# Squares at a layer's end: six of eight blocks added on GpSimd, three tiles summed on TensorE

## The reference

```
def rmsnorm(x, g):
    y = x * rsqrt(mean(x * x, axis=-1) + EPS)
    return y * g

def trunk_layer(x, mod, l, P, ctx):
    h = rmsnorm(x, norm1_g) * (1 + sc1) + sh1
    x = x + g1 * mixer_block(h)
    h = rmsnorm(x, norm2_g) * (1 + sc2) + sh2
    return x + g2 * expert_choice_ffn(h)      # 16 experts, each picks its tokens

y = rmsnorm(x, final_g)                        # after the second layer
```

## Time and profile before

| | us |
|---|---|
| median of 3 runs | 2075.14 (2074.89 to 2081.32) |
| profiled execution | 2075.57 |
| its span (first to last instruction) | 2073.7 |
| TensorE busy | 1896.8 (91%) |
| VectorE, ScalarE, GpSimd busy | 676.0, 378.5, 37.9 |
| end of the first layer: first scatter at 1037.70, q projection starts at | 1051.85 |
| end of the second layer: first scatter at 2054.23, span ends at | 2073.7 |

### The profile page before, as it was taken

How to read it: one execution, slowest core, us unless ns; L and a number is a source line. 1 busy time by engine, 2 the same in 40 slices (tenths; PEclk the granted TensorE clock), 3 DMA queues, 4 the chain that set the end, 5 groups by cost and what they waited for, 6 DMA issues and landing times. The chain is left out here.

```text
span 2073.7 us, 21734 instructions
## 1 busy us (share of the span) xinstructions
PE 1896.8 (91%) x8224; PEld 978.7 (47%) x8224; DVE 676.0 (33%) x1739; ACT 378.5 (18%) x891; POOL 37.9 (2%) x68
## 2 busy tenths in 40 slices
PE   6999989999989899989899999899998998989896
PEld 2445546555544434343354555554655344343432
DVE  1223425544242323231123233353533322232312
ACT  2022312222111110111121223112321011110101
POOL 0000000000000000000000000000000000000000
PEclk9999999999999999999999999999998999999999
DMA  9422341312889999999954214315146899999995
GB/s 362 172 103 102 123 154 61 145 63 102 365 346 428 427 428 427 428 427 428 392 193 163 81 62 147 130 61 188 41 183 263 349 427 427 428 427 428 428 427 216
DMA packets 81655, 547.05 MB, mean 264 GB/s; under 512 B 6992, under 2 KB 10064, under 8 KB 50704
## 3 DMA queue, kind: packets, MB, share of 16 engines
q1 hardware_dynamic: 79104, 536.76, 63.6%
q0 software_dynamic: 2016, 8.06, 1.0%
q10 hardware_dynamic: 432, 0.84, 0.1%
HBM read 541.97 MB, written 3.67 MB: 263 GB/s over the span
## 5 line engine op out<-in xcount | busy, mean ns | idle before, releaser
L865 PE MATMUL bank_D<-HM,ring 128*128 128x384 f32 x1600 | 545.8, 497 | 16.6 <-DMA ring<-w_mgate 4.9
L865 PEld LDWEIGHTS bank_D<-HM,ring 128*128 128x128 f32 x1600 | 302.5, 193 | 235.4 <-issue 38.0
L1310 PE MATMUL bank_D<-ring,HM 128*64 128x512 f32 x912 | 204.8, 596 | 9.8 <-ACT HM L1638 6.6
L871 PE MATMUL bank_D<-ring,HM 128*128 128x512 f32 x384 | 170.1, 597 | 0.0
L1310 PEld LDWEIGHTS bank_D<-ring,HM 128*64 128x64 f32 x912 | 76.0, 138 | 127.7 <-issue 115.6
L1031 PE MATMUL bank_D<-arena_c,ring 128*128 128x384 f32 x384 | 127.3, 488 | 5.0 <-issue 3.1
L871 PEld LDWEIGHTS bank_D<-ring,HM 128*128 128x128 f32 x384 | 71.3, 190 | 86.0 <-issue 84.7
L2226 DVE TENSOR_TENSOR EB<-EB,bank_D 128x512 f32<-128x512 f32 x32 | 22.0, 688 | 267.5 <-ACT EB L1650 267.5
L1334 PE MATMUL bank_Y<-ring,EB 128*64 128x512 f32 x448 | 104.1, 610 | 5.5 <-issue 5.5
L1310 PE MATMUL bank_D<-arena_a,HM 128*64 128x512 f32 x448 | 101.2, 593 | 6.7 <-ACT HM L1638 4.2
L2238 DVE COPY arena_b<-bank_Y 32x512 f32<-32x512 f32 x64 | 44.1, 689 | 176.6 <-PE bank_Y L1334 176.1
(11 more groups left out here) (287 smaller groups left out, 1830.3 us busy)
## 6 DMA issues: line engine op xcount, KB each, us to landing
ring<-ex_w_gate SPq DMA_DIRECT2D x31, 2048.0 KB, 23.2
ring<-ex_w_down SPq DMA_DIRECT2D x28, 2048.0 KB, 19.3
ring<-ex_w_up SPq DMA_DIRECT2D x26, 2048.0 KB, 20.9
ring<-ada_w SPq DMA_DIRECT2D x23, 2048.0 KB, 8.5
ring<-w_in SPq DMA_DIRECT2D x16, 2048.0 KB, 12.7
arena_a<-ex_w_up SPq DMA_DIRECT2D x16, 2048.0 KB, 18.7
arena_a<-ex_w_down SPq DMA_DIRECT2D x15, 2048.0 KB, 23.0
ring<-w_mgate SPq DMA_DIRECT2D x12, 2048.0 KB, 8.1
```

The source lines that it names most:

```text
L865: last = mm(u.t[:, 0:N], w[:, kt, c * P:(c + 1) * P], src[:, kt, :], start=kt == 0, stop=kt == KT - 1)
L871: last = mm(u.t[:, :], HT[:, kt, tile(t)], w[:, kt, 0:CH], start=kt == 0, stop=kt == KT - 1)
L1310: last = mm(u.t[64 * c:64 * c + 64, :], XE[:, h * 4 + k, j, :], w[:, k, c * 512:(c + 1) * 512], start=h == 0 and k == 0, stop=h == 1 and k ...
```

## The change

For the layer's last group the sum steps no longer stand between the scatters: all eight scatters come first, then three sum steps. A new function of GpSimd, add_squares, waits for the second square and adds blocks 0 and 1 into SQ_SUM, then adds blocks 2, 3, 4 and 5 into it, each when its square is done, with a drain between; the last add raises the semaphore pooled. TensorE's first sum step waits for pooled and multiplies SQ_SUM by the ones; the second and third take the blocks 6 and 7 from HT. At the first layer's end add_squares stands behind GpSimd's five DMA issues.

```
+POOLED = 6
     for d in range(KT):
-        s += [("scatter", d)] + ([("sum", d - 2)] if d > 1 else []) 
-    return s + [("sum", KT - 2)] + [("sum", KT - 1)]
+        s += [("scatter", d)]
+    return s + [("sum", d) for d in range(KT - POOLED + 1)]
...
+            def add_squares(l):
+
+                for d in range(1, POOLED):
+                    pool.wait_ge(squares, (l + 1) * KT + d + 1)
+                    last = nc.gpsimd.tensor_tensor(SQ_SUM, HT[:, 0, :] if d == 1 else SQ_SUM, HT[:, d, :], ALU.add)
+                    if d < POOLED - 1:
+                        nc.gpsimd.drain()
+                last.then_inc(pooled, 1)
...
                 pool.dma_start(HS[:, :, :], A["ssm_t"][one].rearrange("a d p n -> p (a d) n")).then_inc(ssm_in, 16)
+                if l:
+                    add_squares(l - 1)
...
                 rstd(RST[:, :], EPS * D).then_inc(token_rstd, 1)
+            add_squares(DEPTH - 1)
...
                 elif kind == "sum":
-                    square_sum(use(here, ("sum", 0)), l + 1, step[1])
+                    u, i = use(here, ("sum", 0)), step[1]
+                    if i == 0:
+                        pe.wait_ge(u.drained, u.before)
+                        pe.wait_ge(pooled, l + 1)
+                    else:
+                        pe.wait_ge(squares, (l + 1) * KT + POOLED + i)
+                    last = mm(u.t[:, 0:N], ones, HT[:, POOLED + i - 1, :] if i else SQ_SUM, start=i == 0, stop=i == KT - POOLED)
+                    if i == KT - POOLED:
+                        last.then_inc(u.filled, 1)
...
-                elif step == ("sum", KT - 1):
+                elif step == ("sum", KT - POOLED):
                     token_rstd(use(here, ("sum", 0)))
```

More of the change, by code:

```diff
@@ L661, in build @@
         aff_ready, picked, weighted, hid_sigmoid = sem("aff_ready"), sem("picked"), sem("weighted"), sem("hid_sigmoid")
-        half_read = sem("half_read")
+        half_read, pooled = sem("half_read"), sem("pooled")
         k_out, v_out, ssm_out, c_out, m_out, y_out = (sem(x) for x in ("k_out", "v_out", "ssm_out", "c_out", "m_out", "y_out"))
```

## The result

The changed kernel takes 2091.62 us (median of 4 runs, 2090.56 to 2093.27), the kernel before 2077.81 us on the same chip (4 runs, 2074.89 to 2081.32). The ratio is 1.0063 with a 95% interval of 1.0041 to 1.0085: slower by some 13 us. The forecast was 2074.7 us, with a range from 2071.0 to 2079.6.

What follows compares the result with a forecast made beforehand. TensorE was taken to set the pace at the layer ends. 1.06 us won less 0.17 lost gave 0.9, less 0.4 for the clock 0.5: 2075.57 to 2075.1, with the median 0.43 lower 2074.7 us, range 2071.0 to 2079.6.

Steps and rivals of the forecast that it cites:

- The adds run from 1042.05 to 1047.05: First layer's end: GpSimd's five adds follow its DMA issues at p = 1.0; Ln at 1049.36, 0.17 us lost.
- p: Time from one GpSimd add to the next: 1.0 us, 0.86 for the add and 0.15 between; balance at 1.09.
- the second layer's gain: Second layer's end: Ln starts at about 2064.66 and not 2065.72, so 1.06 us won.
- VectorE's pace: Layer ends: VectorE's blocks come 0.88 us apart instead of 1.30 once the sums between scatters are gone.
- the way to p = 1.74: GpSimd's adds wait for VectorE's instructions on XT, adding 0.74 us each; a small part of the slower-adds rival's 0.23.
- The rule that the prediction took from the Trainium skill: VectorE hinders GpSimd only with two SBUF inputs or in a two-port mode, so p stays at 1.0.
- The clock: First layer's end: TensorE's new pause may lower the clock for the sums; 0.4 us lost, between 0 and 1.95.
- A time over 2081.4: Whole run slower than 2081.4 us, needing p of about 1.7 or more; chance 0.08.
- adds that are slow in themselves: Rival: GpSimd's adds slower, layer's end waits; from p = 1.09 a loss, 2079.2 us at 1.5; chance 0.23.
- the squares' pace: Rival: p under 0.88, GpSimd's adds keep up with the squares; 3.1 us won, 2072.0 us; chance 0.15.
- the clock alone: Rival: lower-clock stretches after 1050 start or end elsewhere; 5.8 us won to 1.95 lost, likelier 2072 to 2077; chance 0.12.
- my signs of being wrong: TensorE's wait for the adds short or absent, adds starting over 1.2 us apart, or lower-clock stretches changing elsewhere.

Runs made afterwards that it cites:

- e2: Changed kernel with semaphores in place of the drains between GpSimd's adds, five DMAs still ahead of the adds: 2078.13 us, ratio 1.0017 to the kernel before.
- e3: Changed kernel with only one of GpSimd's five DMAs (rows) ahead of the adds at the first layer's end, four behind: 2081.84 us, one run.
- e5: Changed kernel with adds ahead of DMA issues, semaphores for drains, and GpSimd's sum last: 2075.08 us against 2074.37 for the kernel before, ratio 0.9996.
- e6: e5 plus three matmuls of constants behind the first layer's last sum: 2069.86 us against 2074.37 for the kernel before, ratio 0.9975.

## Why the prediction was wrong

**The step that failed** is "The adds run from 1042.05 to 1047.05" at the first layer's end. Its price for the drain between two adds was the 0.15 us of the earlier trace rows. No DMA of GpSimd was under way there (the timeline has the last issue before it 106 us earlier, at 1108.31), but at the first layer's end five were. I named the issues and let them delay the start of the adds by 1.3 us; I did not ask what a drain behind them waits for. The trace before did not show it: in all its 20 pairs of this kind, 0.14 to 0.84 us apart, GpSimd's last issue lies at least 37 us back, and its DMAs land within 14 us. The first drain took 10.2 us. e2 (drain replaced, DMAs kept) and e3 (wait follows the landing of the one DMA left) show it.

**The whole of the first layer's end**, by the profile of the changed kernel: Ln 24.28 us after the first scatter, where the forecast had 11.66. Of these 12.62 us, 10.0 are the hole (10.19 less the 0.15 in the sum), 0.6 the slower adds, and 1.97 the sums at the lower clock.

**p** was 1.11 us, not 1.0: five adds from 2075.61 to 2081.16. An add takes 0.99 to 1.04 us where I had put 0.86. This is a mis-sized term: with a slightly later start of the sums (0.14 us behind the last add, not 0.06) it makes the second layer's gain 0.44 us and not 1.06, and over both ends it alone would have cost 1.1 us. My estimate from the Trainium skill, "GPSIMD Engine Reference", section "Performance versus the Vector engine" (4497 ns for 2048 columns), was 0.84 us an add; the trace has some 0.15 us more.

**VectorE's pace** was right: 0.88 us a block, its last add ends 6.85 us after its first start, to the hundredth. The adds do not hinder it: its pairs take 1.58 us beside them, as in the earlier trace rows. Nor does it hinder the adds: four take 4.41 us beside it at the second layer's end and 4.39 at the first, where it had nothing left to do. So the way to p = 1.74 is ruled out. The rule that the prediction took from the Trainium skill ("SBUF — State Buffer", section "Who interferes with whom") agrees with these numbers.

**The clock** fell in the new pause, at the full price that I had named (4.22 us for the sums where 2.25 had been counted, so 1.97). What came back in the q projection differs between two executions of the same kernel: 0.10 us here (13.50, before 13.60) and 1.35 in the second profile (12.25).

**The rivals.** A time over 2081.4 had a chance of 0.08, and it came, but by neither of the mechanisms that I gave it (adds that are slow in themselves, adds that wait for VectorE). GpSimd didn't keep the squares' pace (1.11 against 0.88), and the clock alone did not decide (1.97 of the 12.62 us). One of my signs of being wrong did show: at the first layer's end the second add starts 11.2 us after the first, where I had named over 1.2 as such a sign.

## What to carry to other kernels

A drain on GpSimd behind DMAs that it has issued can cost until these have landed; order its own arithmetic with semaphores, or ahead of the issues. A price read from a row holds for what was under way beside that row: look at what the same instruction finds in flight at its new place. A pause of TensorE can be paid twice, by its length and by the lower clock of what follows; here three idle matmuls in a pause of 2.7 us gave back 1.4 us of the projection.

## What was not expected of the hardware

- GpSimd's drain waits for GpSimd's own DMAs (10.2 us with five under way, 5.4 with one, 0.24 with none; the wait ends 0.3 to 0.4 us after the last landing in three profiles) and not for SP's: in the changed kernel a load of w_in, issued at 1044.91, was under way until 1064 (19.2 us), the drain was over by 1061.7.
- GpSimd's arithmetic itself runs beside its DMAs: with five under way the first add takes 1.04 us and the next four 4.21 (e2), without 0.99 and 4.22 (e5).
- Three idle matmuls of 0.9 us each in a wait of 2.7 us kept the granted clock at 1.00 through the projection behind it (e6); without them it fell to 0.50 once the projection had begun (e5).
